# Streaming encoder step: two orders of small matmuls in attention, parameters turned in two tiles, and three waits moved at the start

## The reference

```
h = RMSNorm(x);  [x_rec | x_gate | c_q | c_kv | k_rot | g_rec | g_att] = h @ W_in
rec = gelu(x_gate) * RG-LRU(causal_conv4(x_rec))        # log_a = -8 * r * softplus(-lambda)
q = rope(rms(c_q) @ W_uq), then RMS over the 96 of a head;  k from c_kv and k_rot, RMS over the 96
att = softmax(q k^T / sqrt(96), chunk-causal) @ v       # 16 heads, v = ckv_all @ W_uv, 64 wide
x += W_out( sigmoid(g_rec) * rec + sigmoid(g_att) * att )
x += cross attention to 256 memory tokens (4 heads);  x += FFN (layer 0) or top-2-of-8 experts (layer 1)
```

## Time and profile before

| | us |
|---|---|
| median of three runs | 2956.5 |
| lowest, highest | 2948.6, 2964.04 |
| the profiled execution | 2962.77 |
| its span, first to last instruction | 2961.0 |
| PE busy in the span | 2764.7 (93%) |
| DVE, ACT, POOL busy | 1964.3, 1375.8, 311.8 |

### The profile page before, as it was taken

The page is one execution under the profiler, slowest core; times in us unless marked ns, Lnnn a source line. Parts: engine busy times, 40 slices in busy tenths (PEclk is TensorE's granted clock), DMA queues, the critical chain, the costliest instruction groups (busy, mean ns, idle before and its releaser), DMA issues.

```text
span 2961.0 us, 43527 instructions
## 1 busy us (share of the span) xinstructions
PE 2764.7 (93%) x17912; PEld 2539.2 (86%) x17912; DVE 1964.3 (66%) x3354; ACT 1375.8 (46%) x1936; POOL 311.8 (11%) x436
## 2 busy tenths in 40 slices
PE   6999899989999999999999899999998799999997
PEld 5999788779988999999999787779998778888886
DVE  6667677766564534445767777766653588999998
ACT  2343356653343212213344266654332367777774
POOL 2000232320000000000000223220000100000002
PEclk9999899989998999999999899979988799999999
DMA  5322100003331222222222200002331589999996
GB/s 195 105 83 77 37 19 19 1 29 109 107 100 58 72 86 74 84 82 83 77 81 66 61 19 19 1 29 95 108 113 44 192 320 388 388 388 387 388 381 239
DMA packets 220663, 385.25 MB, mean 130 GB/s; under 512 B 35996, under 2 KB 157918, under 8 KB 220465
## 3 DMA queue, kind: packets, MB, share of 16 engines
q1 hardware_dynamic: 205376, 332.23, 32.2%
q0 software_dynamic: 15088, 50.23, 4.8%
HBM read 352.99 MB, written 29.44 MB: 129 GB/s over the span
## 4 chain that ended last, share of the span: by engine, by line
PE 76%; DVE 14%; ACT 7%; issue 2%; POOL 0%; DMA 0%; DVEq 0%; ACTq 0%; POOLq 0%
PE ACC L457 20%; PE ACC L459 19%; PE ACC L458 19%; PE TP L457 4%; PE TP L458 4%; PE TP L459 4%; ACT P L1247 2%; DVE WL L1478 1%; ACT SQT L1247 1%; DVE XC L1694 1%; DVE PTL L1506 1%; PE TP L988 1%; PE TP L673 1%; PE TP L665 1%; DVE WL L2221 1%
## 5 line engine op out<-in xcount | busy, mean ns | idle before, releaser
L457 PE MATMUL ACC<-XH,WH 128*128 128x288 f32 x1984 | 591.6, 298 | 10.1 <-DVE WL L1478 3.6
L459 PE MATMUL ACC<-XH,WL 128*128 128x288 f32 x1984 | 592.1, 298 | 0.0
L458 PE MATMUL ACC<-XL,WH 128*128 128x288 f32 x1984 | 590.8, 298 | 0.0
L2221 DVE TENSOR_TENSOR WL<-MW,WH 128x2048 fp32r<-128x2048 f32 x192 | 436.9, 2289 | 66.0 <-ACT WH L1409 66.0
L1409 ACT ACTIVATE WH<-MW 128x2048 fp32r<-128x2048 f32 x192 | 368.0, 1918 | 138.8 <-PE ACC L459 94.1
L1041 ACT ACTIVATE WH<-RAW 128x2048 fp32r<-128x2048 f32 (+1 forms) x129 | 238.1, 1845 | 337.1 <-PE ACC L459 321.9
L457 PEld LDWEIGHTS ACC<-XH,WH 128*128 128x128 f32 x1984 | 377.3, 190 | 12.7 <-issue 7.0
L458 PEld LDWEIGHTS ACC<-XL,WH 128*128 128x128 f32 x1984 | 376.4, 190 | 0.0
L459 PEld LDWEIGHTS ACC<-XH,WL 128*128 128x128 f32 x1984 | 375.2, 189 | 0.0
L1478 DVE TENSOR_TENSOR WL<-RAW,WH 128x2048 fp32r<-128x2048 f32 (+1 forms) x129 | 284.6, 2206 | 127.8 <-ACT WH L1041 127.6
L457 PE MATMUL ACC<-YH,WH 128*128 128x288 f32 x864 | 259.4, 300 | 5.6 <-DVE YL L1506 3.9
(11 more groups left out here) (490 smaller groups left out, 6143.9 us busy)
## 6 DMA issues: line engine op xcount, KB each, us to landing
MW<-in_moe_w_dram SPq DMA_DIRECT2D x192, 1024.0 KB, 8.3
RAW<-in_w_in_dram SPq DMA_DIRECT2D x36, 1024.0 KB
RAW<-in_ffn_w_dram SPq DMA_DIRECT2D x30, 1024.0 KB
dispatched<-ZT POOLq DMA_DIRECT2D x4, 2048.0 KB, 18.0
RAW<-in_w_out_dram SPq DMA_DIRECT2D x8, 1024.0 KB
RAW<-in_w_mk_dram SPq DMA_DIRECT2D x8, 1024.0 KB
RAW<-in_w_mv_dram SPq DMA_DIRECT2D x8, 1024.0 KB
RAW<-in_w_mq_dram SPq DMA_DIRECT2D x8, 1024.0 KB
```

What stands on the lines that cost most here:

```text
L457: nc.tensor.matmul(out, a[0], b[0], start=first, stop=False)
L458: nc.tensor.matmul(out, a[0], b[1], start=False, stop=False)
L459: return nc.tensor.matmul(out, a[1], b[0], start=False, stop=last)
L2221: v.tensor_tensor(low, MW[raw_place(PLACE[key])][:].rearrange("p j n -> p (j n)"), high.bitcast(F32), ALU.subtract)\
```

## The change

Four edits. (1) PST becomes two tiles of 20 rows; PE turns layer 0's once its own 19 loads are in, and layer 1's after token tile 4; DVE copies each turn to its half of PT, the second after `prepare(5)`. (2) ACT runs one small Square as soon as `ones` is set, ahead of its wait for `params`. (3) ACT's wait for `lam` moves behind the gate banks, the next weight split and the wait for `g_gelu`. (4) In attention the next even head's sums of squares are issued between the products of the next odd head's queries, and the odd head's weighted values and the stream tokens' values alternate, matmul by matmul, into the two halves of one double bank of ring a (`("pv", p)`), where they had two banks of ring b; DVE reads both in `pair_output`.

```diff
@@ attention_order
         a += [("q", even + 2), ("q", odd + 2)] if more else []
+        a += [("pv", p)]
...
-        b += [("pv", odd), ("pvs", p)]
@@ tensor
-            for layer in range(DEPTH):
+            def turn_parameters(layer):
                 pe.wait_ge(s["params%d_in" % layer], PARAM_DMAS // DEPTH * 16)
...
+            turn_parameters(0)
             pe.wait_ge(s["tokens_in"], 32)
             for c in range(C):
...
+                if c == 4:
+                    turn_parameters(1)
@@ tensor, attention
-                def query_half(wq, head, bank, h):
+                def query_half(wq, head, bank, h, between=None):
                     cols = slice(h * HALF, (h + 1) * HALF)
                     for c in range(3):
                         mm = product(...)
+                        if between is not None and 3 * h + c < TT:
+                            between(3 * h + c)
...
+                def square_sum(head):
+                    bank = bank_b(("qs", head))
+                    pe.wait_ge(s["q_sq"], layer * N_HEADS + head + 1)
+
+                    def tile(tt):
+                        mm = nc.tensor.matmul(bank[0:rows(tt), tt:tt + 1], QSQS[layer][head % 2][0:QK, tt * P:tt * P + rows(tt)],
+                                              ones[0:QK, 0:1], start=True, stop=True)
+                        if tt == TT - 1:
+                            mm.then_inc(s["b_ready"], 1)
+                    return tile
...
+                def odd_values(pair):
+
+                    emptied_b(*(("t", 2 * pair + 1, n) for n in range(4)))
+                    emptied_b(("t", 2 * pair, 1))
+                    bank = bank_a(("pv", pair))
+                    for wide, narrow in zip_longest(prompt_products(2 * pair + 1, bank[:, 0]), sample_products(bank[:, 1])):
+                        last = narrow
+                    last.then_inc(s["a_ready"], 1)
...
                     if more:
-                        queries(wq, odd + 2)
-                        query_squares(even + 2)
+                        queries(wq, odd + 2, square_sum(even + 2))
                         query_squares(odd + 2)
                         turn_keys(even + 2)
-                    weighted_values(odd)
-                    sample_values(p)
+                    odd_values(p)
@@ scalar
-            t.skip("tp", 1)
+            t.skip("tp", 2)
+            act.wait_ge(s["consts"], 2)
+            fn(HBT[:, 0, 0:1], ones[:, 0:1], ACT.Square)
             act.wait_ge(s["params"], 1)
...
-                    if i == 0:
-                        if layer == 0:
-                            lambda_exp(0)
-                        act.wait_ge(s["lam"], layer + 1)
+                    if layer == 0 and i == 0:
+                        lambda_exp(0)
...
                     act.wait_ge(s["g_gelu"], t.next("g_gelu").n)
+                    if i == 0:
+                        act.wait_ge(s["lam"], layer + 1)
@@ scalar, values_high
-                        act.wait_ge(s["b_ready"], layer * len(B_AT) + B_AT["pvs", pair - 1] + 1)
+                        act.wait_ge(s["a_ready"], layer * len(A_AT) + A_AT["pv", pair - 1] + 1)
@@ vector
+                def pair_output(pair):
+                    n = layer * len(A_AT) + A_AT["pv", pair]
+                    dve.wait_ge(s["a_ready"], n + 1)
+                    gated(pair, 1, slice(0, SEQ), ACC[:, n % 2, 0, 0:SEQ])
+                    gated(pair, 0, slice(SEQ, T), ACC[:, n % 2, 1, 0:NEW])
+                    gated(pair, 1, slice(SEQ, T), ACC[:, n % 2, 1, NEW:2 * NEW]).then_inc(free_a(n), 1)
@@ gpsimd
-            nc.gpsimd.memset(PST[:], 0.0).then_inc(s["pst"], 1)
+            for layer in range(DEPTH):
+                nc.gpsimd.memset(PST[layer][:], 0.0).then_inc(s["pst"], 1)
```

More of the change, by code:

```diff
@@ L9 @@
 from contextlib import ExitStack
+from itertools import zip_longest
 import concourse.bass as bass
@@ L272, in stream_step_kernel @@
         put = region(W0)
-        PST = put("PST", [DEPTH * ROWS, D])
+        PST = [put("PST%d" % layer, [ROWS, D]) for layer in range(DEPTH)]
         put = region(W0)
@@ L537, in _ @@
             pe.wait_ge(s["consts"], 4)
-            for layer in range(DEPTH):
+            def turn_parameters(layer):
                 pe.wait_ge(s["params%d_in" % layer], PARAM_DMAS // DEPTH * 16)
[L540 to L544, removed]
+                bank = open_tp()
+                for c in range(C):
+                    mm = nc.tensor.transpose(bank[:, c * ROWS:(c + 1) * ROWS], PST[layer][:, c * P:(c + 1) * P], ident[0:ROWS, 0:ROWS])
+                mm.then_inc(s["tp_ready"], 1)
+            turn_parameters(0)
             pe.wait_ge(s["tokens_in"], 32)
@@ L669, in query_squares @@
                 def query_squares(head):
-                    bank = bank_b(("qs", head))
-                    pe.wait_ge(s["q_sq"], layer * N_HEADS + head + 1)
+                    tile = square_sum(head)
                     for tt in range(TT):
-                        mm = nc.tensor.matmul(bank[0:rows(tt), tt:tt + 1], QSQS[layer][head % 2][0:QK, tt * P:tt * P + rows(tt)],
-                                              ones[0:QK, 0:1], start=True, stop=True)
-                    mm.then_inc(s["b_ready"], 1)
+                        tile(tt)
                 def scores(head):
@@ L718, in turn_second, with prompt_products @@
                     turn_probabilities(head, 3, [P23[1][:, k * P:(k + 1) * P] for k in range(4)])
-                def weighted_values(head):
-                    if head % 2 == 0:
-                        pe.wait_ge(s["v_lo"], layer * PAIRS + head // 2 + 1)
+                def prompt_products(head, out):
+                    for j in range(4):
+                        yield from products(out[:, j * P:SEQ], tuple(v[:, j, :, :].rearrange("p a b -> p (a b)") for v in (VH, VL)),
+                                            tuple(p[:, 4 * j:3 * j + 4, :].rearrange("p a b -> p (a b)") for p in (PTH, PTL)), j == 0, j == 3)
@@ new lines, in sample_products, with products @@
+                def sample_products(out):
+                    for k in (1, 2, 3, 4, 0):
+                        n = rows(k + 4)
+                        yield from products(out[:, 0:2 * NEW], tuple(v[0:n, k + 4, :, :].rearrange("p a b -> p (a b)") for v in (VH, VL)),
+                                            (PSH[0:n, k, :], PSLS[layer][0:n, k, :]), k == 1, k == 0)
+                def products(out, a, b, first, last):
+                    yield nc.tensor.matmul(out, a[0], b[0], start=first, stop=False)
+                    yield nc.tensor.matmul(out, a[0], b[1], start=False, stop=False)
+                    yield nc.tensor.matmul(out, a[1], b[0], start=False, stop=last)
@@ L725, in weighted_values, with even_values @@
+                def even_values(head):
+                    pe.wait_ge(s["v_lo"], layer * PAIRS + head // 2 + 1)
                     emptied_b(*(("t", head, n) for n in (0, 2, 3)))
                     bank = bank_b(("pv", head))
-                    for j in range(4):
-                        mm = product(bank[:, j * P:SEQ], tuple(v[:, j, :, :].rearrange("p a b -> p (a b)") for v in (VH, VL)),
-                                     tuple(p[:, 4 * j:3 * j + 4, :].rearrange("p a b -> p (a b)") for p in (PTH, PTL)), j == 0, j == 3)
@@ L730, in weighted_values @@
[L730 to L740, removed]
+                    for mm in prompt_products(head, bank):
+                        last = mm
@@ L764, in _ @@
                     scores(odd)
-                    weighted_values(even)
+                    even_values(even)
                     if more:
@@ L1637, in _, with parameters @@
             step(v.memset(SQ[:], 0.0))
-            bank, m = take_tp()
-            v.tensor_copy(PT[:], bank[:, 0:C * DEPTH * ROWS].rearrange("p (c r) -> p c r", c=C)).then_inc(s["tp_free"], 1)
-            dve.wait_ge(s["tp_free"], m.at(4))
+            def parameters(layer):
+                bank, m = take_tp()
+                v.tensor_copy(PT[:, :, layer * ROWS:(layer + 1) * ROWS], bank[:, 0:C * ROWS].rearrange("p (c r) -> p c r", c=C))\
+                    .then_inc(s["tp_free"], 1)
+                dve.wait_ge(s["tp_free"], m.at(4))
+            parameters(0)
             marker("params").then_inc(s["params"], 1)
@@ L1655, in _ @@
                     split_low()
+                if c == 5:
+                    parameters(1)
             for layer in range(DEPTH):
@@ L1989, in _ @@
                         keys_low(even + 2)
-                    head_output(odd)
-                    sample_output(p)
+                    pair_output(p)
                 gated_sum(PAIRS - 1)
```

31 lines of the change are left out of this document (13 added, 18 removed).

## The result

The changed kernel takes 3060.4 us (median of 4 runs, 3047.3 to 3069.4) against 2954.7 us for the kernel before in the same set: ratio 1.034 [1.031, 1.037], 3.4% slower. The forecast was 2976 with a range to 3003: the direction was right, the size far too small. The profiled execution took 3059.0 us, 3057.3 of it span; its mean granted clock is 0.928, against 0.949 before.

What follows compares the result with a forecast made beforehand. PE was taken to bound the kernel (76% of the chain that ended last). 14 x (1.35 + 0.8) + 2.4 for the stages' ends - 13.1 for the start = +19.4 us: 2976 on the median, range 2942 to 3003.

Steps and rivals of the forecast that it cites:

- The start: Kernel start: earlier PE start 4.6, early table load 0.85 and moved lambda wait 7.7 together save 13.1 us (10.6 to 16).
- PE's first work: Kernel start: with parameters in two tiles PE begins near 14.3 us, 4.6 us earlier than before.
- lambda: First gates: moving ACT's wait for lambda behind the gate banks gives back 7.7 us (6.2 to 7.9).
- The two stands: Attention, 14 pairs: PE stands 2.35 us ahead of the odd head's queries and 0.95 after them, while ACT squares.
- DVE's chain behind E: Attention: from DVE's scaling through means and roots to the keys' low part 6.34 us; keys ready at E + 7.3.
- The squares between the products: Attention, odd head's queries: five squares between wide products add 0.65 us, of a range from 0 to 1.15.
- The full-clock sum: Attention: at full clock each of 14 pairs gets 1.35 us longer (+0.6 to +1.9).
- the 3.4 of the sum: Attention: the alternating values of odd head and stream tokens take PE 3.4 us at full clock.
- The clock: Attention: lower granted clock after the stands adds 0.8 us a pair (-0.5 to +3.4).
- Rival 2: Attention: half clock after every stand, over queries and values, 1.35 + 3.4 us a pair, +56 us, 3012; chance 0.15.
- The stages' ends: End of each attention stage: PE's next unit waits for the last pair's `pair_output`, +1.2 us, twice.

Runs made afterwards that it cites:

- e1: The kernel before with edits 1 to 3 alone (two parameter tiles, early table load, wait for lambda behind the gates): 2941.4 us, ratio 0.995.
- e5_nowait: The kernel before with the even head's squares between the odd head's query products, but written to that head's own bank, without the added wait: 2981.2 us, ratio 1.010.
- e10_whole_filled: The whole change with 16 throwaway products of 288 columns ahead of each of the 14 added waits: 3019.1 us, ratio 1.021.
- e6: e3 with 16 throwaway products of 288 columns ahead of the added wait: 3017.9 us, ratio 1.024.
- e4: The kernel before with the wait moved ahead of the odd head's queries, the squares in a row behind them as before: 3022.0 us, ratio 1.023.
- e7: e4 with 16 throwaway products of 288 columns ahead of the added wait: 2996.0 us, ratio 1.015.
- e3: The kernel before with only the next even head's squares put between the next odd head's query products, the wait ahead of them: 3061.0 us, ratio 1.036.
- e9: The whole change measured again, unaltered, in a second set of runs: 3044.5 us, ratio 1.030.
- e8: The whole change without its squares part (start edits and alternating values, squares in a row after the queries as before): 2942.2 us, ratio 0.996.

## Why the prediction was wrong

**The start: right.** Forecast -13.1, measured -14.5 (the interval allows -7 to -22). The traces say about -11: the first probabilities of layer 0's first odd head are turned at 371.3 to 374.6 in the five kernels with the start's edits, and at 381.8 to 385.2 in the eight with none of them. Inside it PE's first work came at 15.69 and not 14.3 (3.2 us in place of 4.6), and lambda gave 6.5 to 7.0 in place of 7.7. So both small misses are there in the traces. The median's -14.5 can hold spread from elsewhere: in the profiled executions e1's last stretch, which no edit touches, is 11 us shorter than that of before.

**The two stands: right.** 2.16 against 2.35 forecast, 0.89 against 0.95, 14 of each, at the places named.

**DVE's chain behind E, the end of the odd head's queries: right.** 6.36 us from the scaling to the keys' low part against 6.34. In pair 2 the last query product ends at about 476.7 and the keys are ready at 484.07, E + 7.4 against E + 7.3.

**The squares between the products: wrong by 0.65 us a pair.** "I take 0.65" for five, of a range from 0 to 1.15; they cost 1.30 (e5_nowait), over the upper end. The forecast bounded them by wide products with hidden loads on the one side and squares in a row on the other. The product behind a narrow one pays too, 0.22 for 0.13; no row shows it, but the trace of before has it at 466.01, where the first query product behind the transposes takes 0.22 (to 466.23). The earlier trace rows show a narrow one behind wide ones, cheap at 0.03; half of the alternation is the other direction.

**The full-clock sum: +1.35 a pair forecast, about +2.1 measured.** Pair 1 of e10_whole_filled runs at full clock and has A = 433.6 - 417.3 = 16.3, against 13.9, the least of the kernel before: 2.4, of which 0.25 is the fill's, which takes 2.41 (430.76 to 433.17 in e6) for a stand of 2.16. Over the forecast are the squares by 0.65 and the values by 0.4 (429.77 to 433.61, 3.8 for the 3.4 of the sum), under it the stand by 0.2.

**The clock: this is the step that failed.** "I take +0.8 us a pair", with an upper end of +3.4. In the whole change A is 21.5: 7.2 over before, of which 2.1 are the path at full clock. The remaining 5.1 a pair, 71 us in all, are half clock by difference, where 0.8 was forecast. The mean clocks of the two whole executions agree: 0.928 of 3057.3 us is 440 us at half clock, 0.949 of 2961.0 is 302, and 138 us more at half clock cost an estimated 69 if PE is taken as busy in them. The filled kernels show that 1.9 (e4 against e7) to 3.6 (e3 against e6) of the 5.1 hang on the first stand, 3.1 in the whole change (e9 against e10).

The argument for 0.8 was that "wide matmuls now lie between the squares": it had the effect backwards. Behind a stand the alternation makes the half-clock stretch longer (clock 0.60 in e3, 0.71 in e4; no run shows why). Each microsecond by which the queries end later also delays ACT's square and DVE's chain, and in pair 2 PE's remaining work, not DVE's keys, still ends last. The forecast's upper end doubled the queries (+1.9) and a part of the values (+1.5). Pair 2 of the changed kernel against pair 1 of e10, at full clock: queries with squares 6.8 for 3.8, squares in a row 2.1 for 1.2, key transposes 2.1 for 1.6, values 5.7 for 3.8, together 6.3 us. The squares in a row and the key transposes ran at 0.50 in all 14 pairs, the values at 0.64 to 0.87 in all but one.

Rival 2 (half clock after every stand, +56 us, 3012) was the one with the right mechanism, and got 0.15. Even it was low: 14 x (1.35 + 3.4) = 66.5 against 14 x (2.1 + 5.1) = 101. The evidence set against it was one pair of the kernel before, in which queries behind transposes run at full clock. But there PE does not stand between transposes and queries; the rows that had a stand of that length behind transposes were the earlier trace rows, with 0.66. They were read, and priced far below what they say: 0.66 over 15 us is up to 15 x 0.34 = 5.1 us of work lost to the clock (an estimate, with PE taken as busy), and 0.8 was taken.

**The sum now:** 14 x (2.1 + 5.1) - 11 = +90, beside +89 (second set) and +106 (first, with some 13 us more than the second in the last, unedited stretch). The stages' ends (+1.2 twice forecast) were not measured by themselves.

## What to carry to other kernels

Ask of every added wait on the bounding engine what it does to the clock behind it, not only how long it is: here a stand of 2.2 us behind transposes cost 4 to 5 us where the squares followed in a row and 7 to 7.5 where they lay between wide products. A wait that moves ahead of the work which used to cover it is the price of an interleaving; look for the bank's last reader before anything else. If such a stand can't be avoided, work of no use ahead of it can be cheaper than standing (e10 against e9, e7 against e4), and not moving the wait is cheaper still (e8).

## What the runs showed of the hardware that was not expected

- The granted clock need not fall in the stand: in pair 1 of e3_squares it fell 1.3 us after it, at about 438.8, in unbroken products, and the stretch from there to the scores had 0.54. Over the 14 pairs of e3 the fall lies between 1.4 us before the stand's end and 1.9 us behind it; in the changed kernel it lies in the stand in five pairs.
- 16 throwaway products in place of a stand raised the mean clock up to the scores from 0.60 to 0.90 (the throwaway work counted in) and made the kernel some 40 us faster than with the stand, though it had 224 products more to do.
- A one-column float32 square between 288-column products costs about 0.26 us at full clock (1.30 for five): 0.14 for its own two passes, 0.09 on the product behind it, and more at the last one. In a row it is 0.23.
